# Attention probabilities left unnormalised, one decay scan per head pair, value products of two chunks among the levels

## The reference, cut to what matters

```python
def rwkv7_scan(r, decay, k, v, kk, a):
    def step(S, inp):
        r_t, w_t, k_t, v_t, kk_t, a_t = inp
        sa = jnp.einsum('bhij,bhj->bhi', S, -kk_t)
        S = (S * w_t[:, :, None, :]
             + sa[..., None] * (kk_t * a_t)[:, :, None, :]
             + v_t[..., None] * k_t[:, :, None, :])
        return S, jnp.einsum('bhij,bhj->bhi', S, r_t)
    ...
def attend(args):                       # per block of 128 queries
    ...                                 # the 128 keys of highest index score per query
    s = jnp.einsum('bqhr,bqkr->bhqk', qa.astype(f32), c_sel)
    s = jnp.where(valid[:, None], s, -jnp.inf)
    p = jax.nn.softmax(s, axis=-1)
    return jnp.einsum('bhqk,bqkr->bqhr', p, c_sel)
...
o = jnp.einsum('bthr,hrd->bthd', o_lat, w_uv).reshape(B, T, ATTN_WIDTH)
return o * jax.nn.silu(gate)
```

## Time and profile before

| quantity | value |
|---|---|
| median of three runs | 1506.5 us (1506.4 to 1506.83) |
| profiled execution: own time | 1508.41 us |
| profiled execution: span of the records | 1506.6 us |
| granted TensorE clock, mean over the span | 0.954 of full speed |
| busy PE, PEld | 1440.9 us (96%), 1169.9 us (78%) |
| busy DVE, ACT, POOL | 958.8 us (64%), 508.4 us (34%), 487.7 us (32%) |
| projections and key selection | 0 to 174 us |
| attention loop | 174 to 241.3 us |
| substitution, with the value products | 241.3 to 298.3 us |
| levels | 298.3 to 329.1 us |
| scan over the chunks | 329.1 to 375.3 us |
| second block | 375.3 to 1506.6 us |

### The profile page before, as it was taken

One profiled execution on the slowest core, in us unless ns is written; L12 is line 12 of the kernel. 1 busy time (PEld: TensorE's weight loads), 2 busy tenths in 40 slices (PEclk: granted clock), 3 DMA queues, 4 the chain that ended last, 5 costly groups with the idle time before them and its releaser, 6 DMA issues.

```text
span 1506.6 us, 18494 instructions
## 1 busy us (share of the span) xinstructions
PE 1440.9 (96%) x7532; PEld 1169.9 (78%) x7532; DVE 958.8 (64%) x1329; ACT 508.4 (34%) x701; POOL 487.7 (32%) x132
## 2 busy tenths in 40 slices
PE   8999978899998999999999999989989999999997
PEld 6778645787978787788888887768878888888886
DVE  6679856633553565668987975573347888885121
ACT  5443387333233333112222223322234333332121
POOL 0004010002434332243434342334433444343441
PEclk9999898858998999999999999999989999999998
DMA  5221000023232221223232322222231222323221
GB/s 201 84 84 56 29 1 1 1 85 110 87 112 85 89 79 57 84 86 111 84 112 85 112 84 84 84 76 92 85 111 57 95 101 87 110 84 105 84 91 56
DMA packets 21348, 125.12 MB, mean 83 GB/s; under 512 B 2384, under 2 KB 3408, under 8 KB 7696
## 3 DMA queue, kind: packets, MB, share of 16 engines
q1 hardware_dynamic: 20752, 121.71, 23.2%
q10 hardware_dynamic: 512, 2.23, 0.4%
HBM read 121.84 MB, written 2.10 MB: 82 GB/s over the span
## 4 chain that ended last, share of the span: by engine, by line
PE 89%; DVE 7%; ACT 2%; issue 1%; DMA 0%; POOLq 0%; POOL 0%; DVEq 0%; SPq 0%; ACTq 0%
PE bank L394 25%; PE bank L395 24%; PE bank L396 24%; PE bank L346 1%; PE bank L960 1%; PE bank L976 1%; PE bank L376 1%; ACT w_hi L1209 1%; DVE conv_b L2342 1%; PE bank L709 1%; PE bank L579 1%; PE bank L385 1%; PE bank L853 0%; PE bank L746 0%; PE bank L756 0%
## 5 line engine op out<-in xcount | busy, mean ns | idle before, releaser
L1156 POOL TENSOR_TENSOR w_lo<-w_raw,w_hi 128x2048 fp32r<-128x2048 f32 (+1 forms) x102 | 467.1, 4579 | 786.7 <-ACT w_hi L1209 769.1
L394 PE MATMUL bank<-op_hi,w_hi 128*128 128x512 f32 x1344 | 531.1, 395 | 13.8 <-DVE op_lo L1682 6.7
L395 PE MATMUL bank<-op_lo,w_hi 128*128 128x512 f32 x1344 | 527.1, 392 | 0.0
L396 PE MATMUL bank<-op_hi,w_lo 128*128 128x512 f32 x1344 | 526.9, 392 | 0.0
L394 PEld LDWEIGHTS bank<-op_hi,w_hi 128*128 128x128 f32 x1344 | 254.4, 189 | 71.9 <-issue 10.7
L1209 ACT ACTIVATE w_hi<-w_raw 128x2048 fp32r<-128x2048 f32 (+2 forms) x109 | 205.7, 1887 | 282.2 <-PE bank L396 282.1
L396 PEld LDWEIGHTS bank<-op_hi,w_lo 128*128 128x128 f32 x1344 | 254.0, 189 | 54.7
L395 PEld LDWEIGHTS bank<-op_lo,w_hi 128*128 128x128 f32 x1344 | 254.3, 189 | 54.2 <-issue 0.7
L2234 DVE SCALAR_TENSOR_TENSOR bank<-pad_b,par,bank 128x512 f32<-128x512 f32 x232 | 175.3, 756 | 7.8
L2401 DVE TENSOR_TENSOR tmp<-tmp,conv_f 128x512 f32<-128x512 f32 x22 | 101.5, 4615 | 16.4 <-ACT tmp L1628 16.4
L2142 DVE TENSOR_TENSOR x_res<-bank,x_res 128x512 f32<-128x512 f32 x24 | 16.5, 691 | 108.8 <-PE bank L396 108.7
(11 more groups left out here) (365 smaller groups left out, 1783.0 us busy)
## 6 DMA issues: line engine op xcount, KB each, us to landing
w_raw<-in_w_units SPq DMA_DIRECT2D x104, 1024.0 KB, 4.9
w_raw<-in_w_units SPq DMA_DIRECT2D x4, 768.0 KB, 4.2
x_res<-in_x SPq DMA_DIRECT2D x8, 256.0 KB, 6.3
x_res<-in_x ACTq DMA_DIRECT2D x2, 1024.0 KB, 6.6
out<-x_res SPq DMA_DIRECT2D x8, 256.0 KB, 2.3
w_raw<-in_w_units SPq DMA_DIRECT2D x3, 512.0 KB, 8.6
w_raw<-in_w_units SPq DMA_DIRECT2D x4, 256.0 KB, 5.8
mem_tok<-in_mem SPq DMA_DIRECT2D x1, 1024.0 KB, 5.2
```

What stands on the lines that cost most here:

```text
L394: nc.tensor.matmul(b[:, 0:width], h, xh[:, x0 + k, 0:width], start=start and k == ks[0], stop=False)
L395: nc.tensor.matmul(b[:, 0:width], h, xl(x0 + k, width), start=False, stop=False)
L396: mm = nc.tensor.matmul(b[:, 0:width], l, xh[:, x0 + k, 0:width], start=False, stop=stop and k == ks[-1])
L1156: nc.gpsimd.tensor_tensor(w_lo[u % 2][:, 0:nk, :], w_raw[u % 2][:, 0:nk, :], w_hi[u % 2][:, 0:nk, :].bitcast(F32), ALU.subtract).then_inc( ...
```

## The change

**Attention.** `probabilities` and its semaphore `prob_ready` go; the transposes wait for `exp_ready`, and the unnormalised exponentials are turned and multiplied with the values. DVE inverts the sums into `inv_mass` (row maxima, sums and inverses now have two copies each, in a new tile `soft`). PE's `heads_out(p)` gets eight more matmuls, which spread the inverses over 64 partitions a head, query along the free axis (a column of `inv_mass` broadcast against the identity, as `norms_spread` does), into a bank of their own, `mass`. DVE's `heads_out` multiplies `gate_a` by that bank first, and then by the bank `o`.

**Decay.** `key_terms` makes one scan over all 512 tokens into `prep[3]` and takes each chunk's middle value off in four `tensor_scalar` of 129 columns, in place of four linked scans, a copy and a `tensor_tensor` of 516 columns.

**Order.** In the attention loop `head_inputs(p)` now stands right before `scores(p)`, behind `heads_out(p - 2)` of the pass before; before it stood ahead of `heads_out`. ACT's `exps(p)` comes last in its pass. DVE's substitution is cut into three pieces (0 to 8, 8 to 16, 16 to 31), with only the `value_grams` of chunks 0 and 1 between. `token_major`, `value_grams` and `chunk_values` of chunks 2 and 3 move behind the substitution, among the levels; the `output_gram` of chunks 2 and 3 move behind the last `corners`.

The diff, cut:

```diff
+MASS_ORDER = [(odd, q) for q in range(NT) for odd in range(2)]
...
+        soft = at("soft", S0 + 5632, [48])
+        inv_mass = [soft[:, 32 + 8 * s:40 + 8 * s] for s in range(2)]
...
             def probabilities_turned(p):
                 for n, (odd, q) in enumerate(TILES):
-                    pe.wait_ge(sem("prob_ready"), 2 * NT * p + n + 1)
+                    pe.wait_ge(sem("exp_ready"), 2 * NT * p + n + 1)
                     transposes(("pT", p, odd, q), [prob[p % 2][odd][q][:, k * P:k * P + P] for k in range(q + 1)])
...
                 done(mm, ("o", p))
+                b = bank(("mass", p))
+                pe.wait_ge(sem("mass_inverted"), p + 1)
+                for odd, q in MASS_ORDER:
+                    n = TILES.index((odd, q))
+                    mm = nc.tensor.matmul(b[HD * odd:HD * odd + HD, q * P:q * P + P], inv_mass[p % 2][:, n:n + 1].to_broadcast([P, HD]),
+                                          ident[:, :], start=True, stop=True)
+                done(mm, ("mass", p))
...
-            attention_start()
-            for p in range(NI - 1):
-                scores(p + 1)
-                strict_upper(p + 1)
-                if p + 2 < NI:
-                    decay_and_rate(p + 2)
-                    norms_spread(p + 2)
-                probabilities_turned(p)
-                if p + 2 < NI:
-                    head_inputs(p + 2)
-                else:
-                    pe.wait_ge(sem("prep_ready"), NI)
-                    pe.wait_ge(sem("bk_decayed"), 2 * NI)
-                    token_major(0)
-                    value_grams(0)
-                heads_out(p)
-                if p + 2 < NI:
-                    key_bonus(p + 2)
-
-            def chunk_values(c, between=None):
+            pe.wait_ge(sem("dsa_w"), 16 * 3)
+            evacuated(pe, "rs_kv")
+            head_inputs(0)
+            decay_and_rate(1)
+            norms_spread(1)
+            scores(0)
+            strict_upper(0)
+            head_values()
+            key_bonus(1)
+            for p in range(1, NI):
+                head_inputs(p)
+                scores(p)
+                if p + 1 < NI:
+                    decay_and_rate(p + 1)
+                    norms_spread(p + 1)
+                strict_upper(p)
+                if p + 1 < NI:
+                    probabilities_turned(p - 1)
+                    heads_out(p - 1)
+                    key_bonus(p + 1)
...
+            pe.wait_ge(sem("prep_ready"), NI)
+            pe.wait_ge(sem("bk_decayed"), 2 * NI)
+            token_major(0)
+            probabilities_turned(NI - 2)
+            value_grams(0)
+            heads_out(NI - 2)
             chunk_values(0)
             probabilities_turned(NI - 1)
             token_major(1)
             value_grams(1)
             heads_out(NI - 1)
-            for c in range(1, NT):
-                chunk_values(c)
-                if c + 1 < NT:
-                    token_major(c + 1)
-                    value_grams(c + 1)
+            chunk_values(1)
             pe.wait_ge(sem("blocks_out"), 2)
             side_products(0)
             side_products(1)
+            token_major(2)
+            value_grams(2)
             side_blocks(0)
             side_blocks(1)
-            for c in (0, 2):
-                upper_halves(c)
-                upper_halves(c + 1)
-                output_gram(c)
-                corners(c)
-                corners(c + 1)
-                output_gram(c + 1)
+
+            def first_halves():
+                token_major(3)
+                upper_halves(0)
+                upper_halves(1)
+
+            chunk_values(2, first_halves)
+            value_grams(3)
+            corners(0)
+            corners(1)
+
+            def second_halves():
+                upper_halves(2)
+                upper_halves(3)
+                output_gram(0)
+
+            chunk_values(3, second_halves)
+            output_gram(1)
+            corners(2)
+            corners(3)
+            output_gram(2)
+            output_gram(3)
...
-            def probabilities(p):
-                act.wait_ge(sem("sums_inverted"), p + 1)
-                for n, (odd, q) in enumerate(TILES):
-                    t = prob[p % 2][odd][q][:, :]
-                    A(t, t, ACT.Copy, scale=rsum[:, n:n + 1]).then_inc(sem("prob_ready"), 1)
...
-            for p in range(NI - 1):
-                exps(p + 1)
-                strict_upper(p + 1)
-                if p + 2 < NI:
-                    decay_and_rate(p + 2)
-                turned(p)
-                if p + 2 < NI:
-                    decays(p + 2)
-                    head_inputs(p + 2)
-                    probabilities(p + 1)
+            for p in range(1, NI):
+                head_inputs(p)
+                if p + 1 < NI:
+                    decay_and_rate(p + 1)
+                strict_upper(p)
+                if p + 1 < NI:
+                    turned(p - 1)
+                    decays(p + 1)
+                    exps(p)
...
                 evacuated(dve, ("z", i))
-                if i:
-                    link(V.memset(cum[:, :, 0:1], 0.0))
+                running = prep[3][:, 0:T + 1]
+                link(V.memset(running[:, 0:1], 0.0))
+                link(V.tensor_tensor_scan(running[:, 1:T + 1], ones[:, 0:1].to_broadcast([P, T]), prep[0][:, 0:T], 0.0, ALU.add, ALU.add))
                 for c in range(NT):
-                    ins = V.tensor_tensor_scan(cum[:, c, 1:P + 1], ones[:, :], prep[0][:, c * P:c * P + P], 0.0, ALU.add, ALU.add)
-                    link(ins)
-                link(V.tensor_copy(mid, cum[:, :, HD]))
-                V.tensor_tensor(cum, cum, mid.unsqueeze(2).to_broadcast([P, NT, P + 1]), ALU.subtract)\
-                    .then_inc(sem("cum_ready"), 1)
+                    span = running[:, c * P:c * P + P + 1]
+                    ins = V.tensor_scalar(cum[:, c, :], span, running[:, c * P + HD:c * P + HD + 1], None, ALU.subtract)
+                ins.then_inc(sem("cum_ready"), 1)
...
             def probs(p):
                 dve.wait_ge(sem("exp_ready"), 2 * NT * (p + 1))
-                V.reciprocal(rsum[:, :], sums[:, :]).then_inc(sem("sums_inverted"), 1)
+                V.reciprocal(inv_mass[p % 2], mass[p % 2]).then_inc(sem("mass_inverted"), 1)
 
             def heads_out(i):
+                b = take(dve, ("mass", i))
+                evac(V.tensor_tensor(gate_a[:, i, :], b[:, :], gate_a[:, i, :], ALU.mult), ("mass", i))
+                evacuated(dve, ("mass", i))
                 b = take(dve, ("o", i))
                 evac(V.tensor_tensor(gate_a[:, i, :], b[:, :], gate_a[:, i, :], ALU.mult), ("o", i))
...
-            probs(0)
-            for p in range(NI - 2):
-                maxima(p + 1)
-                if p:
-                    heads_out(p - 1)
-                key_terms(p + 2)
-                probs(p + 1)
-                decayed(p + 2)
+            for p in range(1, NI - 1):
+                if p >= 2:
+                    heads_out(p - 2)
+                maxima(p)
+                probs(p - 1)
+                key_terms(p + 1)
+                decayed(p + 1)
+            heads_out(NI - 3)
             maxima(NI - 1)
-            heads_out(NI - 3)
+            probs(NI - 2)
             blocks_in()
-            substitution(0, 4)
+            substitution(0, 8)
             probs(NI - 1)
-            substitution(4, 10)
             value_grams(0, 0)
             value_grams(0, 1)
             heads_out(NI - 2)
-            substitution(10, 14)
+            substitution(8, 16)
             value_grams(1, 0)
             value_grams(1, 1)
             heads_out(NI - 1)
-            substitution(14, 20)
-            value_grams(2, 0)
-            value_grams(2, 1)
-            substitution(20, 26)
-            value_grams(3, 0)
-            value_grams(3, 1)
-            substitution(26, BLK - 1)
+            substitution(16, BLK - 1)
...
+            value_grams(2, 0)
+            value_grams(2, 1)
...
             corner_parts(1)
-            for c in (0, 2):
-                upper_halves(c)
-                upper_halves(c + 1)
+            upper_halves(0)
+            upper_halves(1)
+            value_grams(3, 0)
+            value_grams(3, 1)
+            upper_halves(2)
+            upper_halves(3)
+            for c in range(NT):
                 output_gram(c)
-                output_gram(c + 1)
```

More of the change, by code:

```diff
@@ L222, in build @@
         probT = [at(f"probT{odd}", 16384 + 8192 * odd, [NT, T]) for odd in range(2)]
+        soft = at("soft", S0 + 5632, [48])
+        peak = [soft[:, 8 * s:8 * s + 8] for s in range(2)]
+        mass = [soft[:, 16 + 8 * s:24 + 8 * s] for s in range(2)]
+        inv_mass = [soft[:, 32 + 8 * s:40 + 8 * s] for s in range(2)]
         gn_tok = at("gn_tok", R0, [NI * 2 * NT])
@@ L601, in scores @@
                                 done(mm, ("s", p, odd, j))
-            def attention_start():
-                decay_and_rate(1)
-                norms_spread(1)
```

(34 more changed lines are left out.)

9 lines of the change are left out of this document (4 added, 5 removed).

## The result

| kernel | median | runs |
|---|---|---|
| before | 1506.45 us | 1503.11 to 1506.83, 4 |
| changed | 1496.09 us | 1492.17 to 1498.92, 4 |

What follows compares the result with a forecast made beforehand. Bounds: ACT and PE in attention, DVE in substitution, PE at half clock in the levels. 1508.4 - 6.7 - 10.6 + 24.9 - 1.3 - 3.0 = 1511.7 us profiled, so 1509.5 forecast; range 1494 to 1516.

Steps and rivals of the forecast that it cites:

- Loop: Attention loop: without ACT's copies, scores of pair 3 start 6.7 us earlier (2.2, 0.5 and 4.0 by pass).
- `mass` and the second gate multiplication: Attention heads: matmuls about 1.0 us and DVE multiplication 0.69 a pair; DVE's wait for mass(3) 1.8.
- Substitution: From scores of pair 3 to side_products: DVE's chain 10.6 us shorter, fewer value_grams and waits; blocks_in keeps its 3.20.
- Rival C: Substitution: DVE's gate multiplications wait for mass(3), side_products starts at 286, total 1514.5 us; chance 0.15.
- some clock: ... I take 3 us for that: Levels: moved wide matmuls should bring full clock for a while, credited with 3 us.
- what the levels take on: Levels: moved value work adds 24.9 us at half clock, less 1.3 idle and 3 for clock, net 20.6.
- rival B: Levels: moved full-column work brings full clock back, 1489.5 to 1496.5, taken as 1494 us; chance 0.23.
- The scan: Behind the levels: length unchanged, clock rise left at 347; a chunk earlier or later worth 3 us either way.
- that nothing shortens: Scan's start: DVE and ACT chain from g_b at 329.20 to first state product at 335.25, with mem_tok 2.19 us.

Runs made afterwards that it cites:

- copies_back: Changed kernel with ACT's 32 normalising copies put back, mass matmuls and second gate multiplication taken out; 1506.6 us, ratio 0.9985 to the kernel before.
- move_only: Kernel before with only the value work of chunks 2 and 3 moved among the levels; 1507.1 us, ratio 0.9987 to the kernel before.
- scans_back: Changed kernel with four linked scans, the copy and the 516-column subtraction in place of one scan and four subtractions; 1500.5 us, ratio 0.9941 to before.
- late_mem: Changed kernel with ACT's table load, square root and two mem_tok scalings moved behind its first scan_u copies; 1486.0 us, ratio 0.9852 to before.
- tokens_early: late_mem with the 20 transposes of chunks 2 and 3 moved out of the levels into PE's wait for the substitution; 1486.1 us, ratio 0.9863 to before.
- all_of_it: filled and tokens_early together, with 10 extra matmuls ahead of the levels in place of 14; 1480.6 us, ratio 0.9821 to before.
- values_back: Changed kernel with the value work of chunks 2 and 3 put back beside the substitution; 1497.7 us, ratio 0.9913 to the kernel before.
- warm_back: values_back with 4 extra unread 128x512 matmuls in PE's wait ahead of side_products; 1494.0 us, ratio 0.9910 to the kernel before.
- back_late: values_back with late_mem's ACT order; 1498.5 us, ratio 0.9936 to the kernel before.
- warm_late: Changed kernel with the edits of warm_levels and late_mem together; 1480.4 us, ratio 0.9819 to the kernel before.
- filled: warm_late with 3 more unread 128x512 matmuls ahead of the second side_blocks; 1480.0 us, ratio 0.9817 to the kernel before.
- warm_levels: Changed kernel with 14 extra unread 128x512 matmuls while PE waits for the substitution to end; 1492.0 us, ratio 0.9897 to the kernel before.

## Why the prediction was wrong

- **Loop**, 6.7 forecast, 6.1 measured: right in sum, by luck in its parts. For 2.2, 0.5 and 4.0 us the scores show a loss of 1.2 (199.28, 198.1 before), then gains of 3.0 and 4.3. The clock's fall in the first pass was there, 187.6 to 191. copies_back puts 9.5 us of the result on the ACT copies, net of the `mass` matmuls and the second gate multiplication.
- **`mass` and the second gate multiplication** cost what was forecast (1.04 to 1.07 and 0.69 us), and what waits for them waits 0.8 (1.8 forecast).
- **Substitution**, 10.6 forecast, 13.3 measured: sizes. DVE waited 1.1 for the exponentials (2.1 forecast) and 0.35 ahead of `blocks_in`, where I had left 3.20 standing. Rival C didn't happen: the clock was full from 191 to 269.5.
- **The step that failed** is "some clock: ... I take 3 us for that" in what the levels take on: net 20.6 forecast, 10.6 measured, 10 of the 13 us of the miss. The 10.6 is of one execution; in copies_back's, with the same PE order, the levels took 8.2 us less. The terms themselves (24.9 us at half clock) held where the clock was at half: `value_grams(3)` took 3.79, forecast 3.7, and `key_values(2)` 1.12, forecast 0.9. What failed is that it would be at half. I had the mechanism as rival B at 0.23 and judged it by the wrong row: value products (128x64) held 0.50 for 4.6 us, and I let them speak for the `value_grams`, which I called 128x256 (they are 64x256), and of which no stretch at half clock was in the trace of before. The row for it was there as well: a full clock right behind transposes alone, 207.5 to 210.5, and 20 transposes were to move into the levels.
- **What brought the clock back.** In all seven traces with `value_grams(2)` in the levels and half clock ahead of it (changed, move_only, copies_back, scans_back, late_mem, tokens_early, all_of_it) the clock rises in them or within 0.5 us of their end; in the four without (before, values_back, warm_back, back_late) it doesn't rise within the levels at all. Only tokens_early and all_of_it have `value_grams(2)` without transposes right ahead; in move_only, copies_back and scans_back the rise came 0.2 to 0.7 us after its start, so there the transposes may have brought it. In late_mem and warm_late a second rise (296.0, 295.3) came without `value_grams`, behind value products and 8 transposes. What is shown is that the moved work brings the clock back, not that one kind of it must.
- **The scan**, unchanged forecast, 0.5 measured: right in sum by two errors. It began at full clock, lost it in the 3.96 us of waiting for ACT's `mem_tok` (1.51 before, where PE came to it at half clock), and paid with 13 us at half clock. That is where the second half of the levels' gain went: values_back against the changed kernel is nothing, back_late against late_mem is 12.7 us. I had called that chain one "that nothing shortens"; late_mem took it away for 10.6 us.

The Trainium skill, "TensorE: Matmul & The Clock Gate", section "Why this matters for your kernels", wants TensorE kept busy without gaps; filled agrees (PE busy 143.7 of the 156 us from 191 to 347, clock 1.00), warm_back doesn't (busy 25.0 of 26.3, clock 0.50): in these levels being busy was not enough.

The gap of 1.4 to 1.9 us in `side_blocks` goes with the fall in every trace that has the value work in its levels: six have it and fall (changed, scans_back, warm_levels, late_mem, warm_late, tokens_early), four don't and hold (move_only, copies_back, filled, all_of_it). Open is what makes the gap, and why the fall lasted 13 to 14 us in some executions (changed, warm_levels, tokens_early) and 3 to 4 in others (scans_back, late_mem, warm_late). The clock goes with the spread between executions of one kernel, though where it turned in those without a profile is not known: the changed kernel's four took 1498.9, 1497.4, 1494.7 and 1492.2 us at mean clocks of 0.965, 0.966, 0.969 and 0.971.

## What to carry to other kernels

Where a stage runs at half clock, price moved work twice, at either clock, and ask what the trace shows PE doing ahead of each rise, and whether the moved work holds that; here 33.3 us held old and moved work together, where the old alone had taken 30.9. Then look at what stands behind: here gaps of 1.4 to 4 us were followed by a fall, and one of them ate the gain until the wait itself was taken out. In such a kernel compare edits by the mean of several executions, since one profile can differ from another by 8 us in a stage that the edit between them doesn't touch (the levels of the changed kernel and of copies_back).

## What the runs showed of the hardware

- Blocks of 32x32 and 64x64 kept a full clock (296 to 315.3 in late_mem, mixed with wider work), but with `output_gram` (64x128) as the only other work they did not raise one: 0.50 for 26 to 31 us with PE busy 95% and more (before, values_back, warm_back, back_late).
- A gap of 1.4 to 1.9 us among 32x32 blocks came with a fall to half clock, from 0.4 us ahead of its end to 2.0 us behind it, in seven traces (the six above and warm_back).
- Matmuls of 128x512 whose product nobody reads kept the clock up, and cost nothing where they ended before PE's wait did: warm_levels started `side_products` at 278.89, the changed kernel at 278.88. Where they ended 1.75 us too early (all_of_it) the clock fell all the same.
